# Gated-delta decay differences from cumulated log gates kept as rows, in a two-layer mixer kernel on one core

## What is computed

```
def gated_delta_chunked(q, k, v, g, beta):        # g = log gate
    cum = jnp.cumsum(g, axis=-1)                   # within a chunk
    diff = cum[..., :, None] - cum[..., None, :]
    d_incl = jnp.exp(jnp.where(incl, diff, -jnp.inf))
    a_mat = beta[..., :, None] * einsum(k, k) * d_strict
    gam = jnp.exp(cum)
    rhs = concatenate([beta * v, (beta * gam) * k])
    sol = triangular_solve(a_mat, rhs, unit_diagonal=True)
    p_intra = einsum(q, k) * d_incl
    q_g = q * gam
    k_d = k * exp(cum[-1:] - cum); g_end = exp(cum[-1])
    # then, chunk after chunk: u = u0 - w s; o = q_g s + p_intra u
    # s = g_end s + k_d u
```

## Time and profile before

| | us |
|---|---|
| median of three runs | 4124.77 (4124.39 to 4125.28) |
| the profiled execution's own time | 4153.67 |
| its span, first to last instruction | 4151.9 |
| gdn_front of the first layer | 448 to 592 |
| gdn_chunk of the first layer | 592 to 902 |
| both in the second layer | 1753 to 2216 |

### The profile page before, as it was taken

One profiled execution on the slowest core, in us unless ns is written; L12 is line 12 of the kernel. 1 busy time (PEld: TensorE's weight loads), 2 busy tenths in 40 slices (PEclk: granted clock), 3 DMA queues, 4 the chain that ended last, 5 costly groups with the idle time before them and its releaser, 6 DMA issues. The chain is left out here.

```text
span 4151.9 us, 54632 instructions
## 1 busy us (share of the span) xinstructions
PE 3748.6 (90%) x22216; PEld 2359.1 (57%) x22216; DVE 2281.8 (55%) x3988; ACT 1318.5 (32%) x2209; POOL 268.4 (6%) x233
## 2 busy tenths in 40 slices
PE   8868988979999949898898998899999999799998
PEld 4447536766644437744775664476676776344443
DVE  2475367745653366157764664266666767533353
ACT  3253353334543234144423445311111111231003
POOL 0010100000000011010000000111112222000000
PEclk9979998989999979699987998999999999999999
DMA  4213212120043122212112012211111110312231
GB/s 152 82 48 100 73 36 76 59 104 9 9 152 127 58 60 89 76 31 61 49 58 96 11 62 103 72 31 36 41 41 36 41 36 11 125 57 61 90 115 53
DMA packets 279832, 272.74 MB, mean 66 GB/s; under 512 B 12304, under 2 KB 252048, under 8 KB 279584
## 3 DMA queue, kind: packets, MB, share of 16 engines
q1 hardware_dynamic: 279584, 269.26, 19.8%
HBM read 195.88 MB, written 73.33 MB: 65 GB/s over the span
## 5 line engine op out<-in xcount | busy, mean ns | idle before, releaser
L3255 DVE SCALAR_TENSOR_TENSOR cv<-glu,params,cv 128x1024 f32<-128x1024 f32 x240 | 338.2, 1409 | 6.1
L1415 PE MATMUL ps<-hT,w_cols 128*128 128x512 f32 x576 | 254.6, 601 | 13.2 <-PEq L156 13.2
L397 PE MATMUL ps<-hT,w_cols 128*128 128x512 f32 x448 | 203.5, 615 | 3.2 <-PEq L156 3.2
L1415 PEld LDWEIGHTS ps<-hT,w_cols 128*128 128x128 f32 x576 | 110.9, 193 | 152.0 <-issue 150.1
L3553 PE MATMUL ps<-hT,wr 128*128 128x512 f32 x360 | 161.7, 592 | 0.0
L397 PEld LDWEIGHTS ps<-hT,w_cols 128*128 128x128 f32 x448 | 87.8, 197 | 115.7 <-issue 115.5
L3077 PE MATMUL ps<-w_i,hT 128*128 128x128 f32 x1152 | 132.6, 275 | 0.0
L3077 PEld LDWEIGHTS ps<-w_i,hT 128*128 128x128 f32 x1152 | 130.6, 192 | 0.0
L3231 POOL TENSOR_TENSOR Sp<-Sp,Rp 128x520 f32<-128x520 f32 (+1 forms) x56 | 88.4, 1579 | 639.3 <-DVE W L3272 639.3
L3061 PE MATMUL ps<-hT,w_f 128*128 128x347 f32 x384 | 116.2, 462 | 6.6 <-DMA w_f<-in_w_in 6.6
L3068 PE MATMUL ps<-hT,w_q 128*128 128x512 f32 x256 | 111.9, 595 | 9.1 <-DVE attn L3280 9.1
(11 more groups left out here) (901 smaller groups left out, 7656.2 us busy)
## 6 DMA issues: line engine op xcount, KB each, us to landing
w_cols<-in_w_in SPq DMA_DIRECT2D x32, 512.0 KB, 3.8
wr<-in_w_in SPq DMA_DIRECT2D x24, 512.0 KB, 5.0
hT_hbm<-hT SPq DMA_DIRECT2D x2, 4096.0 KB, 15.7
hT<-hT_hbm SPq DMA_DIRECT2D x2, 4096.0 KB, 13.4
fh<-hT_hbm SPq DMA_DIRECT2D x16, 512.0 KB, 4.6
fh_again<-hT_hbm SPq DMA_DIRECT2D x16, 512.0 KB, 4.5
x<-in_x SPq DMA_DIRECT2D x8, 512.0 KB, 10.5
ahead<-kb_hbm SPq DMA_DIRECT2D x16, 256.0 KB, 3.2
```

Of the source, the lines that this page charges most:

```text
L397: q = pe.matmul(ps[:, proj_bank(n, b), :], lhsT=wc[:, n % 3, k, :], rhs=hT[:, k, P + b * 512:P + (b + 1) * 512], start=(k == 0), stop=(k = ...
L1415: q = pe.matmul(ps[:, proj_bank(n, b), :], lhsT=wc[:, n % 3, k, :], rhs=hT[:, k, P + b * 512:P + (b + 1) * 512], start=(k == 0), stop=(k = ...
L3255: vec.scalar_tensor_tensor(out=cv[:, h % 2, :], in0=src, scalar=w, in1=cv[:, h % 2, :], op0=ALU.mult, op1=ALU.add).then_inc(*VEC(f"tap{h}_ ...
```

## The change

It computes cum[i] - cum[j] instead of summing the gates between two tokens.

- In gdn_front, TensorE adds `row_sums`: 32 products of 128 columns with weights 4 or 2 columns wide, after `gate_sums`, which give the cumulated gates with the units on partitions (4 and 2 units of each direction at partitions 0, 32, 64 and 96). ScalarE copies them to `cum_rows` (four copies of 1024 elements), SyncE stores them in HBM, and VectorE builds constant rows (`selectors`).
- In gdn_chunk, a product of `diff` now has five rows: four rows of cum against minus one at the unit, and a row of ones against the unit's cum as a row, which a transfer from HBM brings (`line_rows`). The widths, 512 and 256 columns, stay. The two products stand on different groups of 32 rows of TensorE.
- The difference is positive above the diagonal, so VectorE takes the minimum with zero (`not_above`, from PSUM into `DT`) before ScalarE's Exp, which now works in place in SBUF. `gates` and `Gm` are gone.
- `decays` becomes two products of 384 columns with two rows each, from rows that a transfer brings (`piece_rows`).
- VectorE's order in both first loops is another, and so is one place in ScalarE's.

```
+                cum_rows = sbuf(st, "cum_rows", [P, SEQ])
+                lines = sbuf(st, "cum_lines", [P, 2, 4, P])
+                halves = sbuf(st, "half_rows", [P, P])
+                PARTS = [(0, 0, 4), (0, 4, 2), (1, 0, 4), (1, 4, 2)]
...
+                            if n == 3:
+                                sp.wait_ge(*ACT["rows"])
+                                for r, (e, u0, nu) in enumerate(PARTS):
+                                    sp.dma_start(cum_hbm[GH * e + u0:GH * e + u0 + nu, :], cum_rows[32 * r:32 * r + nu, :]).then_inc(*DMA("cum"))
+                        sp.wait_ge(*DMA["cum"])
...
+                        def row_sums():
+                            for t in range(NT):
+                                for r, (e, u0, nu) in enumerate(PARTS):
+                                    q = pe.matmul(ps[32 * r:32 * r + nu, 4 + t // 4, P * (t % 4):P * (t % 4) + P],
+                                                  lhsT=gb[:, t, 0, GH * e + u0:GH * e + u0 + nu], rhs=cst("tri_b" if e else "tri_f"), start=True, stop=True)
+                            q.then_inc(*PE("rows"))
...
+                        def rows_of_sums():
+                            act.wait_ge(*PE["rows"])
+                            act.wait_ge(*VEC["cum_rows"])
+                            for r, (e, u0, nu) in enumerate(PARTS):
+                                q = act.copy(cum_rows[32 * r:32 * r + nu, :].rearrange("p (b n) -> p b n", b=2), ps[32 * r:32 * r + nu, 4:6, :])
+                            q.then_inc(*ACT("rows"))
...
+                        def selectors():
+                            vec.memset(cum_rows[:, :], 1.0).then_inc(*VEC("cum_rows"))
+                            vec.tensor_tensor(nth[:, :], ident[:, 0:32], ident[:, 32:64], ALU.add).then_inc(*VEC("nth0"))
+                            for n in (1, 2):
+                                vec.wait_ge(*VEC[f"nth{n - 1}"])
+                                vec.tensor_tensor(nth[:, :], nth[:, :], ident[:, 32 + 32 * n:64 + 32 * n], ALU.add).then_inc(*VEC(f"nth{n}"))
+                            vec.wait_ge(*VEC["nth2"])
+                            for b in range(2):
+                                vec.tensor_scalar(lines[:, b, :, :], col(nth[:, 0:4], P), -1.0, None, ALU.mult)
+                            vec.tensor_copy(halves[:, :].rearrange("p (h n) -> p h n", h=2), col(nth[:, 0:2], 64)).then_inc(*VEC("halves"))
...
-                    Gm = hflat[:, 7680:9216].rearrange("p (u n) -> p u n", u=12)
+                    pieces = hflat[:, 7680:8448].rearrange("p (a m n) -> p a m n", a=2, m=3)
...
-                                    pe.wait_ge(*ACT["DT" + old[1:]])
+                                    pe.wait_ge(*VEC["low" + old[1:]])
...
                             def diff(s, e):
-                                pe.wait_ge(*VEC[f"Gm{s}_{e}"])
+                                pe.wait_ge(*DMA.upto(f"lines{s % 2}", 4 * (s // 2 + 1)))
                                 b = claim(f"d{s}_{e}")
-                                g = Gm[:, 6 * e:6 * e + 6, :].rearrange("p u n -> p (u n)")
-                                behind = cst("bef" if e else "aft")
-                                pe.matmul(ps[:, b, :], lhsT=behind, rhs=g[:, 0:512], start=True, stop=True)
-                                pe.matmul(ps[:, b + 1, 0:256], lhsT=behind, rhs=g[:, 512:768], start=True, stop=True).then_inc(*PE(f"d{s}_{e}"))
+                                for half, nu in ((0, 4), (1, 2)):
+                                    r = 32 * (2 * e + half)
+                                    q = pe.matmul(ps[:, b + half, 0:nu * P], lhsT=cum_rows[r:r + 5, tok(s, e)],
+                                                  rhs=lines[r:r + 5, s % 2, 0:nu, :].rearrange("p u n -> p (u n)"), start=True, stop=True)
+                                q.then_inc(*PE(f"d{s}_{e}"))
...
                             def decays(s):
+                                pe.wait_ge(*DMA.upto(f"pieces{s % 2}", 2 * (s // 2 + 1)))
                                 b = claim(f"gam{s}")
-                                for em in range(6):
-                                    e, m = em // 3, em % 3
-                                    for h in range(2):
-                                        g = gb[:, chunk(s, e), 0, GH * e + 2 * m + h:GH * e + 2 * m + h + 1].broadcast_to([P, GD])
-                                        q = pe.matmul(ps[64 * h:64 * h + 64, b + em // 4, (em % 4) * P:(em % 4) * P + P], lhsT=g,
-                                                      rhs=cst("tri_b" if e else "tri_f"), start=True, stop=True)
+                                for e in range(2):
+                                    r = 32 * (2 * e + 1)
+                                    q = pe.matmul(ps[:, b + e, 0:3 * P], lhsT=halves[r:r + 2, :], rhs=pieces[r:r + 2, s % 2, :, :].rearrange("p m n -> p (m n)"),
+                                                  start=True, stop=True)
...
                             def decay_pairs(s, e):
-                                act.wait_ge(*PE[f"d{s}_{e}"])
-                                if s > 4:
-                                    act.wait_ge(*VEC[f"PT{s - 5}_1"])
-                                act.activation(DT[:, s % 5, 6 * e:6 * e + 6, :], units(pair_of_banks(f"d{s}_{e}"), 6, P), FN.Exp).then_inc(*ACT(f"DT{s}_{e}"))
+                                act.wait_ge(*VEC[f"low{s}_{e}"])
+                                act.activation(DT[:, s % 5, 6 * e:6 * e + 6, :], DT[:, s % 5, 6 * e:6 * e + 6, :], FN.Exp).then_inc(*ACT(f"DT{s}_{e}"))
...
                                 decays(s + 1)
                                 decay_pairs(s + 4, 0)
                                 first_half(s)
+                                across(s)
                                 decay_pairs(s + 4, 1)
-                                across(s)
                                 if s == 0:
...
-                            def gates(s, e):
-                                if s:
-                                    vec.wait_ge(*PE[f"d{s - 1}_{e}"])
-                                vec.tensor_tensor(Gm[:, 6 * e:6 * e + 6, :], col(gb[:, chunk(s, e), 0, GH * e:GH * e + GH], P), rep(cst("tri_b" if e else "tri_f"), 6),
-                                                  ALU.mult).then_inc(*VEC(f"Gm{s}_{e}"))
+                            def not_above(s, e):
+                                vec.wait_ge(*PE[f"d{s}_{e}"])
+                                if s > 4:
+                                    vec.wait_ge(*VEC[f"PT{s - 5}_1"])
+                                vec.tensor_scalar(DT[:, s % 5, 6 * e:6 * e + 6, :], units(pair_of_banks(f"d{s}_{e}"), 6, P), 0.0, None,
+                                                  ALU.min).then_inc(*VEC(f"low{s}_{e}"))
...
-                            gates(0, 0)
-                            gates(0, 1)
+                            not_above(0, 0)
+                            not_above(0, 1)
                             for s in range(4):
                                 decay_pairs(s, 0)
-                                gates(s + 1, 0)
+                                if s < 3:
+                                    not_above(s + 1, 0)
                                 decay_pairs(s, 1)
-                                gates(s + 1, 1)
-                                for n in range(2):
-                                    key_pairs(s, n)
+                                key_pairs(s, 0)
+                                if s < 3:
+                                    not_above(s + 1, 1)
+                                key_pairs(s, 1)
                             decays(0)
                             inverses(0)
                             join(0)
                             for s in range(4):
                                 right_side(s)
                                 old_state(s)
+                                not_above(s + 4, 0)
+                                first_half(s)
+                                not_above(s + 4, 1)
+                                across(s)
                                 decays(s + 1)
-                                first_half(s)
+                                keys(s)
                                 decay_pairs(s + 4, 0)
-                                across(s)
-                                keys(s)
-                                decay_pairs(s + 4, 1)
                                 second_half(s)
                                 query_pairs(s, 0)
+                                decay_pairs(s + 4, 1)
                                 new_state(s)
                                 query_pairs(s, 1)
                                 if s == 0:
                                     rest_of_own(0)
                                 key_pairs(s + 4, 0)
-                                if s < 3:
-                                    gates(s + 5, 0)
-                                    gates(s + 5, 1)
                                 out(s)
```

(25 more changed lines are left out.)

9 lines of the change are left out of this document (8 added, 1 removed).

## The result

The changed kernel takes 4230.88 us where the kernel before took 4124.58 beside it; both are medians of four runs. Of the changed kernel's four, one was slow (11876.14 us, at a granted clock of 0.319) and stands in that median but not in the ratios, and the other three took 4213.94, 4225.11 and 4236.64 us. The ratio is 1.0229, 95% interval 1.0177 to 1.0281. That is about 95 us slower (0.0229 x 4124.58; the middle one of the three lies 100.5 above 4124.58), three times the 31 of the forecast, and outside its range. The profiled execution has a span of 4234.7 us.

A forecast was written before the change was run, and what follows sets the result against it. TensorE was taken to bound gdn_front, no single engine the ring, a chain the first loop. 3.9 + 4.0 + 9.0 - 1.3 = 15.6 us a layer, 31.2 in two, gave 4156.0 us; own range 4143 to 4170, widened to 4134 to 4177.

The forecast's parts named there:

- The limits of the stages: gdn_front bound by TensorE; start of gdn_chunk a ring of no engine; first loop a chain, 20.41 us a step.
- Part 1, gdn_front, +3.9: gdn_front: the 64 passes of row_sums add 3.9 us a layer on TensorE, at 61 ns a pass.
- the lower bound I gave: gdn_front: row_sums costs 2.0 us if four strips of 32 run side by side.
- the two-strip row: Old decays in gdn_chunk: 24 passes of 128 columns on 64-wide strips, 61 ns a pass, used to price row_sums.
- Part 2, the start: Start of gdn_chunk: TensorE's first product +2.6 us after four transfers, first key_pairs +2.9.
- Part 2, the ring, +0.5 a turn: First 47 us of gdn_chunk: a turn between engines takes 0.5 us more than 8.8, three times, +1.5.
- the risk in a bracket: Start of gdn_chunk: +4.0 us could be 2 to 7, more with the clock at 1.2 GHz.
- Part 3, the first loop, +9.0: Steps 0 to 3 of gdn_chunk: VectorE's queue makes out_of_state 2.25 us later a step, +9.0 (0 to 12).
- Part 4, the second loop, -1.3: Steps 4 to 7 of gdn_chunk: shorter decays save 0.45 us in each of three steps, -1.3.
- The direction, slower: Whole kernel: slower at 0.81, same 0.15, faster 0.04.
- the clock: Rival: waiting lowers the clock in the first loop too, one fall of 8 us a layer, 4172; chance 0.18.
- row groups don't run side by side: Rival: diff costs 1.3 us and row_sums 7.1, in gdn_front and gdn_chunk, 4174; chance 0.12.

The follow-up runs named there:

- Experiment 1: Kernel before, with the two products of every decay difference in gdn_chunk on five of the 128 rows, other rows left out of the sum; ratio 1.0108, 4170.41 us.
- experiment 6: Changed kernel with another VectorE order in the ring: both decay_pairs ahead of the next minimum, second direction's minimum behind the second key_pairs; ratio 1.0153, 4211.89 us.
- experiment 4: Kernel before, with VectorE's and ScalarE's first loop in the changed kernel's order, products as before; ratio 1.0078, 4174.73 us.
- the kernel with both repairs: Changed kernel with VectorE's order moved in ring and first loop, and differences over 128 rows, 123 of them zeros; ratio 1.0056, 4163.92 us.
- the last run but one of experiment 8: Kernel before, with chunk decays as two-row products and ScalarE's take_out of the second direction one step later in the first loop; ratio 0.9941, 4116.13 us.

## Why the prediction was wrong

*The limits of the stages.* Right: a ring that belongs to no engine, a loop in a chain. But the 20.4 us a step that the forecast started from are those of step 2 alone; steps 0 and 1 took 23.2 and 21.6, step 0 at a clock of 0.86.

*Part 1, gdn_front, +3.9.* Too high: 1.4 in the first layer. The 64 passes of `row_sums` went from 474.4 to 476.1, about 2.0 us with the last pass:

```profile
L1441 PE MATMUL ps<-consts,gb x64: 271/272/273, 474.4 to 476.1; 128*4 128x128 f32 x32, 128*2 128x128 f32 x32
```

That is the lower bound I gave, four strips side by side. I took the two-strip row as "the same kind", though it was not. The second layer shows 3.6, of which 1.6 isn't `row_sums` and is not explained.

*Part 2, the start.* Right, near enough: the first product came 3.9 us after the stage's first issue (predicted 3.7), the minimum took 0.96, and the first `key_pairs` came 13.8 us into the stage (predicted 12.6; 9.8 before).

```profile
606.71 2.08 PE L1699 MATMUL ps<-cum_lines,cum_rows 5*128 5x512 f32 x8 [10.03 <-DMA cum_lines<-cum_hbm]
```

*Part 2, the ring, +0.5 a turn.* **A step that failed.** My chain was the right chain, `key_pairs` to `key_pairs`, but with TensorE's four links at 2.4 GHz: 0.6, 1.0, 1.2 and 1.0 us. They took 1.22, 2.07, 2.08 and 2.07, together 3.6 us more, which is all of what the turn is over the predicted 9.3. I had noted the risk in a bracket and priced it up to 7 for the whole part; the ring cost 13. Experiment 1 shows why the clock sank from 0.76 to 0.50, experiment 6 that another order makes the turn 9.8 even so.

*Part 3, the first loop, +9.0.* **The step that failed most.** The mechanism was right: the queue on VectorE, `out_of_state` waiting for `query_pairs`, no wait for gam in front of `decays`. Its size at 2.4 GHz was about right too, as far as one step shows it (2.5 in experiment 4, whose products are the old ones, against 2.25). But the steps grew by 6.3 to 9.4 us, not by 2.25. The rest, some 4 to 7 us a step, goes with the clock (0.61 to 0.68 in these steps), which I kept at the 1.00 of the earlier trace rows although I had just taken work from TensorE and given it waits.

*Part 4, the second loop, -1.3.* Near, and partly by luck. In the first layer three steps of it together took 58.7 us (885.8 to 944.5) where they took 59.9 (830.2 to 890.1), 1.2 less. But it isn't 0.45 in each: two steps took 17.2 and 17.1 us in place of 18.3, and the one between them 24.4 in place of 23.3. The clock differs as well, 0.74 and 0.83 over the three, and the stage as a whole kept its 74.8 us. One of the shorter steps:

```profile
885.80:903.00 17.20, 17.20 (x230) 14.67 (x226) 10.40 (x17) 6.63 (x10) 0.00 (x0) 0.82 0.04 13
```

*The rivals.* The direction, slower, came out as forecast, but two thirds of the size lay outside the sum. Of the rivals the clock was the right one, mis-sized twice: I counted one fall of 8 us a layer, and it fell in every step and stayed down in all of the ring. And I looked at waiting only. That five rows in place of 128 could matter for the clock never came up, in the sum or in a rival. That row groups don't run side by side is refuted: both halves of a five-row `diff` end in 2.07 us at 1.2 GHz, where 128 rows take 2.93 (593.47 to 596.40 in the kernel before).

*What bears it.* The stages account for the difference: 1.4 + 13.0 + 29.9 + 0.1 in the first layer and 3.6 + 12.9 + 25.4 - 10.7 in the second. Together 75.6 us of the 82.8 between the two spans. The last term is a slow stretch of the second loop that the kernel before had and the changed one hadn't, so one execution doesn't say what it is worth; and 9 us lie ahead of gdn_front (it begins at 457.3 in place of 448.3), in code that the change doesn't touch. What stays open is why the loop of the kernel with both repairs is 5 to 6 us over before, what makes the clock fall in one step and not in a like one, and what exact share of the changed kernel's loop is rows and what waiting. Put into the kernel before one at a time, rows give +12.3 and order +17.4, together 29.7 of the changed kernel's +29.9 (29.0 against +25.4 in the second layer). Taken out of the changed kernel one at a time, the rows give back 1.1 and the orders 16.3. So neither has a fixed share.

## What to carry to other kernels

A product on few rows (5 here) may cost the clock what it saves in work, busy as TensorE looks in it: look at the granted clock of the stretch before trusting a chain of rows read at 2.4 GHz. Price a chain at both levels if the change takes rows, products or continuity from TensorE; a chain that crosses TensorE four times doubles four links. When VectorE's order has to change, place what TensorE waits for ahead of what it doesn't: here moves in the order alone, with the few rows kept, took the ratio from 1.0229 to 1.0056.

## What the runs showed of the hardware

- How many rows a product uses counts for the clock, and zeros in one of its operands don't: 5 rows, ring at 0.51 and +1.08%; 128 rows of which 123 are zeros, 0.74 and +0.16% (interval across zero). No run has a count between 32 and 128. 32 rows did no better than 5 in the changed kernel (0.52), where the waits were there as well. A busy row in a trace isn't yet activity that holds the clock: in experiment 1 the engine is busy 44.4 of 49.5 us in the ring, where it was 32.9 of 47, and has the lower clock. Part of that busy time is the low clock itself, which makes the same passes longer, but it is busy for 18.0 of 18.0 us from 603 to 621 and doesn't get 2.4 GHz in them. The Trainium skill, TensorE: Matmul & The Clock Gate, Part 1, lets the gate go by how busy the engine has lately been; by the busy time of the profile this case disagrees, and the measurement decides.
- Four strips of 2 or 4 columns run side by side (`row_sums` of the changed kernel): 64 passes of 128 columns in about 2.0 us, 31 ns a pass, where two strips of 64 took 61.
- Two-row products of 384 columns took 0.91 us for four passes on two row groups in one stretch at 2.4 GHz, close to the three passes' 1.0 that the forecast worked out for them (the last run but one of experiment 8, which beats the kernel before):

```profile
756.51 0.91 PE L1722 MATMUL ps<-pieces_g,half_rows 2*128 2x384 f32 x4
```
